# State-space layer: the inputs' products ahead of the output scalings; layer norms that subtract the mean first

## What is computed

```python
def _layer_norm(x, g, b):
    mu = jnp.mean(xf, -1, keepdims=True)
    var = jnp.mean(jnp.square(xf - mu), -1, keepdims=True)
    return ((xf - mu) * lax.rsqrt(var + LN_EPS)) * g + b

def _ssd_mixer(h, ...):
    z, xBC, dt = jnp.split(h @ in_w, ...)
    xBC = jax.nn.silu(_causal_depthwise_conv(xBC, conv_w, conv_b))
    xs, Bm, Cm = jnp.split(xBC, ...)
    y = _ssd_chunked(xs * dt[..., None], dt * A, Bm, Cm)
    y = y + xs * D_skip[:, None]
    y = y * jax.nn.silu(z)
    yg = yg * lax.rsqrt(jnp.mean(jnp.square(yg), -1) + RMS_EPS)     # 8 groups of 512 channels
    return (yg * norm_g) @ out_w
```

## Time and profile before

| | |
|---|---|
| three runs | 3546.73, 3548.98, 3554.34 us; median 3548.98 |
| the profiled execution | 3549.42 us, its span 3547.6 us, granted TensorE clock 0.995 |
| TensorE matmul / weight load busy | 97% / 95% |
| VectorE, ScalarE, GpSimd busy | 78%, 56%, 17% |
| DMA | 197 GB/s mean |

### The profile page before, as it was taken

How to read it: one execution, slowest core, us unless ns; L and a number is a source line. 1 busy time by engine, 2 the same in 40 slices (tenths; PEclk the granted TensorE clock), 3 DMA queues, 4 the chain that set the end, 5 groups by cost and what they waited for, 6 DMA issues and landing times.

```text
span 3547.6 us, 68240 instructions
## 1 busy us (share of the span) xinstructions
PE 3447.0 (97%) x27858; PEld 3381.8 (95%) x27858; DVE 2783.1 (78%) x4529; ACT 1987.5 (56%) x3204; POOL 587.2 (17%) x546
## 2 busy tenths in 40 slices
PE   7999999999999999999999999999999998999997
PEld 7999999999999998999999999999999998999997
DVE  7788888577797887877888887898989867666665
ACT  6555546566547676565555546665656746434344
POOL 2111112111113011131111112231313300000000
PEclk9999999999999999999999999999999999999999
DMA  6555556444465444655555565556464543555552
GB/s 239 217 197 219 217 227 231 176 155 179 165 251 203 172 169 173 267 185 218 201 221 202 208 262 180 178 175 230 171 233 169 186 169 146 210 189 199 204 190 107
DMA packets 113688, 699.61 MB, mean 197 GB/s; under 512 B 13216, under 2 KB 29792, under 8 KB 31456
## 3 DMA queue, kind: packets, MB, share of 16 engines
q1 hardware_dynamic: 104128, 685.14, 52.2%
q10 hardware_dynamic: 8784, 8.46, 1.0%
q0 software_dynamic: 464, 1.64, 0.1%
HBM read 684.64 MB, written 2.16 MB: 194 GB/s over the span
## 4 chain that ended last, share of the span: by engine, by line
PE 49%; DVE 13%; ACT 6%; issue 2%; DMA 1%; POOL 1%; DVEq 0%; SPq 0%; POOLq 0%; ACTq 0%
PE g L446 15%; PE g L448 15%; PE g L447 15%; DVE w_lo L1594 4%; ACT w_hi L1026 2%; DMA w_raw<-in_slots 1%; POOL scratch L2409 1%; DVE vec L2095 1%; DVE rstd L2095 1%; PE turn_bank L485 1%; DVE scratch L1659 1%; DVE scratch L2121 0%; DVE scratch L2129 0%; PE norm_bank L459 0%; DVE h L2225 0%
## 5 line engine op out<-in xcount | busy, mean ns | idle before, releaser
L1594 DVE TENSOR_TENSOR w_lo<-w_raw,w_hi 128x1024 fp32r<-128x1024 f32 x1088 | 1337.0, 1232 | 433.9 <-ACT w_hi L1026 423.1
L1026 ACT ACTIVATE w_hi<-w_raw 128x1024 fp32r<-128x1024 f32 x1088 | 1129.6, 1053 | 873.2 <-PE g L448 761.7
L446 PE MATMUL g<-p_hi,w_hi 128*128 128x256 f32 x4576 | 1318.0, 288 | 36.4 <-DVE w_lo L1594 23.2
L448 PE MATMUL g<-p_hi,w_lo 128*128 128x256 f32 x4576 | 1296.2, 283 | 0.0
L447 PE MATMUL g<-p_lo,w_hi 128*128 128x256 f32 x4576 | 1296.2, 283 | 0.0
L446 PE MATMUL g<-q_hi,w_hi 128*128 128x256 f32 x3408 | 980.0, 288 | 5.7 <-DVE w_lo L1594 2.2
L448 PE MATMUL g<-q_hi,w_lo 128*128 128x256 f32 x3408 | 964.0, 283 | 0.0
L447 PE MATMUL g<-q_lo,w_hi 128*128 128x256 f32 x3408 | 963.8, 283 | 0.0
L446 PEld LDWEIGHTS g<-p_hi,w_hi 128*128 128x128 f32 x4576 | 879.1, 192 | 46.1 <-DVE w_lo L1594 32.7
L447 PEld LDWEIGHTS g<-p_lo,w_hi 128*128 128x128 f32 x4576 | 879.3, 192 | 1.4
L448 PEld LDWEIGHTS g<-p_hi,w_lo 128*128 128x128 f32 x4576 | 879.0, 192 | 0.0
(11 more groups left out here) (445 smaller groups left out, 3929.2 us busy)
## 6 DMA issues: line engine op xcount, KB each, us to landing
w_raw<-in_slots SPq DMA_DIRECT2D x640, 1024.0 KB, 4.9
scratch<-scratch SPq DMA_DIRECT2D x128, 64.0 KB, 4.9
scratch<-s_rows ACTq DMA_DIRECT2D x16, 256.0 KB, 3.4
con<-s_rows ACTq DMA_DIRECT2D x16, 256.0 KB, 5.1
h<-in_x SPq DMA_DIRECT2D x4, 512.0 KB, 6.2
out_h<-h SPq DMA_DIRECT2D x4, 512.0 KB, 2.6
sq<-in_p POOLq DMA_DIRECT2D x4, 256.0 KB, 3.0
con<-in_consts SPq DMA_DIRECT2D x1, 832.0 KB, 10.7
```

Of the source, the lines that this page charges most:

```text
L446: pe.matmul(g, wh, hi[:, k], start=n == 0, stop=False)
L448: last = pe.matmul(g, wl, hi[:, k], start=False, stop=n == len(ks) - 1)
L1026: act.activation(w_hi[k % SPLIT][:, cols], raw[MAIN_AT[k] % RAW][:, cols], ACT.Copy).then_inc(hi_ready, 1)
L1594: dve.tensor_tensor(w_lo[k % SPLIT][:, cols], raw[MAIN_AT[k] % RAW][:, cols], w_hi[k % SPLIT][:, cols], SUB).then_inc(lo_ready, 1)
```

## The change

It has two parts.

1. In `s_group` on VectorE, step 6 now runs `s_inputs` and the clamp first and `s_scale_y` behind them, and step 7 runs `s_y_lo` behind its own `s_inputs` and clamp, no longer at its head. This holds for groups 1 to 7.
2. In `layer_norm`, the subtraction comes first and takes the mean straight from `rope_bank`. Five tiles are subtracted between the variance and the wait for `rstd`. Then each tile is multiplied by `rstd`; tiles 5 to 15 are subtracted (with a wait for its end) right before. The one product of mean and `rstd` is gone, and `low` runs one tile behind where it ran two behind.

```diff
+LN_AHEAD = 5
...
         def s_group(g):
             for n in range(10):
-                if g and n == 7:
-                    s_y_lo(g - 1)
                 begin()
...
                 lo_half(1)
-                if g:
+                if g and n < 6:
                     s_previous(g - 1, n)
                 if 4 <= n <= 7:
                     s_inputs(g, n - 4)
...
                     s_clamp(n, s_z[:, n - 6])
+                if g and n > 5:
+                    s_previous(g - 1, n)
+                if g and n == 7:
+                    s_y_lo(g - 1)
...
             dve.tensor_tensor(rsn[:, 1], bN[:, 0:SEQ], rsn[:, 0], SUB).then_inc(ln_var, 1)
+            for n in range(LN_AHEAD):
+                link(dve.tensor_tensor(h[:, n], h[:, n], bR[:, 0:SEQ], SUB))
             factor()
-            link(dve.tensor_tensor(rsn[:, 2], bR[:, 0:SEQ], rstd[:], MUL))
...
             for n in range(DT):
-                link(dve.tensor_tensor(h[:, n], h[:, n], rstd[:], MUL))
-                dve.tensor_tensor(h[:, n], h[:, n], rsn[:, 2], SUB).then_inc(ln_z, 1)
-                if w == 0 and n > 1:
-                    low(n - 2)
+                if n >= LN_AHEAD:
+                    link(dve.tensor_tensor(h[:, n], h[:, n], bR[:, 0:SEQ], SUB))
+                dve.tensor_tensor(h[:, n], h[:, n], rstd[:], MUL).then_inc(ln_z, 1)
+                if w == 0 and n:
+                    low(n - 1)
             if w == 0:
-                low(DT - 2)
                 low(DT - 1)
```

## The result

The changed kernel takes **3556.3 us** (median of 11 runs, 3552.4 to 3560.7); the kernel before takes 3549.0 in the same session (11 runs, 3546.7 to 3554.3). The ratio is **1.0021, 95% interval 1.0014 to 1.0029**, that is 5 to 10 us slower. The forecast was 3555.7 us, between 3551.0 and 3559.5, and +6.7 us. The profiled execution has a span of 3552.1 us, where that of before has 3547.6: 4.5 us more.

The account below looks back on a forecast made before the run. TensorE, 97% busy, was taken as the bound, with ScalarE's chain from the scalings pacing the state-space layer. Part 1 +7.0, first norm +1.2, last norm -1.6: +6.6, rounded up to +6.7, so 3555.7 us, range 3551.0 to 3559.5.

Parts of the forecast that it names:

- The stall and what replaces it: State-space layer: TensorE's seven 1.52 us stalls at `turn_bank` go; about 2.9 us at step 3 without projection instead of 0.5.
- The scalings' customer: Step 6: ScalarE waits for the scaled tiles, so it and the decay-row loads behind it start 1.36 us later.
- The collision moves along: Step 6, VectorE against GpSimd: the input product loses the 0.49 us and the scalings get it back.
- The four boundaries without projection: Between groups: the chain arrives 0.96, 1.18, 1.01 and 1.36 us later, together 4.5 us.
- less the idle time at step 1: Boundaries without projection: VectorE's idle 0.40, 0.18, 0.35 and 0 us at step 1 is taken off the 1.36 us delay.
- The two with a projection: After groups 2 and 4: TensorE waits for VectorE's copies, so each boundary adds 1.36 us, together 2.7.
- After group 7: Boundary behind the last group: TensorE starts 0.15 us behind the copy, 0.2 us earlier than before.
- The low part at nothing: Step 7: moving `s_y_lo` costs nothing, hidden by VectorE's wait at step 8; otherwise 1.14 us at each group.
- The first norm: Part 2, first layer norm: last `q_hi` about 20.8 us after the variance starts, two late tiles in 2.39; +1.2 us.
- The last norm: Part 2, last layer norm: 11.70 us from `rstd` on instead of 13.26, all on the path to the end; -1.6 us.
- The first: Rival: ScalarE's chain has at least 2.9 us of slack between scalings and step 3, giving 3538 us; chance 0.10.
- The third: Rival: chain closed on VectorE and ScalarE through `w_hi` at step 1, nothing absorbed; +9.1 us, 3558.1 us; chance 0.20.

Follow-up runs that it names:

- e4: Kernel before with VectorE's step 6 running scalings, then input products, ahead of the second half of `w_lo`: +3.0 us, ratio 1.0007.
- e7: Kernel before with the scalings ahead of both halves of `w_lo` at step 6 and the products ahead of the second: -2.0 us, ratio 0.9993.
- e3: Kernel before with VectorE's step 6 running input products, then scalings, ahead of the second half of `w_lo`: -2.1 us, ratio 0.9992.
- e5: e1 with the low part back at the head of step 7; against the kernel before: 3555.1 us, ratio 1.0015.
- e2: The change without its `s_group` part, only the layer norms changed; against the kernel before: 3547.3 us, ratio 0.9997.
- e1: The change without its `layer_norm` part, only the state-space layer changed; against the kernel before: 3556.7 us, ratio 1.0026.
- e10: e4 with the 1 MB weight load held until the decay rows have landed; against the kernel before: 3540.8 us, ratio 0.9979.
- e6: Kernel before with a layer norm that subtracts two tiles ahead of `rstd` and runs `low` two behind: 3546.4 us, ratio 0.9992.
- e8: e7 with the layer norm of e6; against the kernel before: 3544.3 us, ratio 0.9985.
- e11: e8 with e10's hold on the weight load; against the kernel before: 3537.1 us, ratio 0.9967.
- e9: Kernel before with the 1 MB weight load of step 6 delayed to just ahead of the decay-row fetch: 3567.8 us, ratio 1.005.
- e12: The changed kernel with the weight load of step 7 held until the decay rows have landed; against the kernel before: 3554.3 us, ratio 1.0017.

## Why the prediction was right

- **The stall and what replaces it.** Right. The stall's rows are gone and the output product waits 2.24, 2.24, 2.23 and 1.30 us at the four boundaries without projection; the last is the one ahead of which the clock had fallen. I had put it at about 2.9 with the restart; from start to start it is 2.5 at the first three.
- **The scalings' customer.** Right to 0.01: the fetch is issued 31.28 us after the output product for 29.93, +1.35 where the text had 1.36. e4 and e7, where the scalings come sooner, are the other side of it (28.79 and 28.51).
- **The collision moves along.** Right for this order: 0.83 for the product and 1.67 for the scalings. The product ends at 2325.78, just behind GpSimd's (2323.86 and 1.77 us, to 2325.63), so the trace agrees with the rule of the Trainium skill ("SBUF — State Buffer", "Who interferes with whom"). But the place behind a half of `w_lo`, to which the prediction tied it, is not the condition. In e3 and e4 the copy stands directly ahead; e3's product starts just ahead of GpSimd's and is not hit, nor are its scalings behind it, while e4's scalings, which run beside GpSimd's product, are (step 6, first e3, then e4):

```profile
2323.25 0.34 DVE L2116 TENSOR_SCALAR scratch<-rstd,vec 128x256 f32<-128x256 f32 x1
2323.30 0.90 POOL L2508 TENSOR_TENSOR vec<-vec,sin_b 128x256 f32<-128x256 f32 x1 [4.70 <-ACT sin_b L1072]
2324.41 1.66 DVE L2129 SCALAR_TENSOR_TENSOR scratch<-scratch,vec,rsn 128x256 f32<-128x256 f32 x4
...
2322.89 2.15 DVE L2129 SCALAR_TENSOR_TENSOR scratch<-scratch,vec,rsn 128x256 f32<-128x256 f32 x4
2322.93 1.03 POOL L2508 TENSOR_TENSOR vec<-vec,sin_b 128x256 f32<-128x256 f32 x1 [4.69 <-ACT sin_b L1072]
```

- **The four boundaries without projection.** Sum 3.8 for 4.5. The step that is off is "less the idle time at step 1". The true slack is the landing-to-product time less 31.5: 0.88, 0.64, 0.82 and 0.46, not 0.40, 0.18, 0.35 and 0; some of it lies behind step 1. The slack is 2.8 in sum where 0.93 was taken, an error of 1.9 us. Of this, 1.2 were given back by things that the sum didn't have: the fetch, taken as it was (3.13 us), changed by +0.36, +0.84, +0.06 and -0.31, and the fallen clock put the last issue 0.3 later. At boundary 3: 1.35 + 0.84 - 0.64 = 1.55, as measured. That the two errors cancel is luck.
- **The two with a projection.** +1.19 and +1.11 for 1.36 each: the 1.35 of the later issue, less 0.12 and 0.22 by which the fetch happened to be shorter. The first wait is now at the projection's first tile, not at the fifth that I had read.
- **After group 7.** -0.34 for -0.2, but not where it was forecast. The tile of the earlier trace rows starts 42.81 us behind the output product, for 42.80 before: nothing is gained there, because the fetch of this group took 3.57 us for 3.23. In e5, where it took 3.29, the tile starts at 42.56, which is the -0.2 of the text. The -0.34 arises behind it, mostly at the norm's last mean product, ahead of which TensorE waited 0.17 us before and doesn't now, and 0.1 of it belongs to part 2, in e2 as well. So the agreement of this number is luck too.
- **The low part at nothing.** Right (e5: same issue of the fetch).
- **The first norm.** Right: from the variance (2946.42) to the last `q_hi` (2967.22) it is 20.80 us, the 20.8 of the text, and two late tiles take 2.38 for 2.39.

```profile
2946.42 0.42 DVE L2220 TENSOR_TENSOR rsn<-norm_bank,rsn 128x256 f32<-128x256 f32 x1 [0.78 <-ACT rsn L1443]
...
2967.22 0.59 ACT L1449 ACTIVATE q_hi<-h,vec 128x256 fp32r<-128x256 f32 x1
...
2971.61 0.36 PE L448 MATMUL g<-q_hi,w_hi 128*128 128x256 f32 x1 [2.32 <-DVE scratch L2309]
```

- **The last norm.** -1.7 for -1.6.
- **The rivals.** The first (slack that I don't see) fell: there were 0.5 to 0.9 us a boundary where 2.9 were needed. The third comes nearest in part: its closed chain is there, but it runs through the fetch and the output product, not through `w_hi` at step 1, and the slack did absorb a part.

The sum of the terms as measured in the trace is +5.4 us, the forecast +6.7, and the medians say +7.4. The profiled execution is one of several, and two things differ from one to the next: the fetches, between 3.2 and 5.9 us, and the granted clock. In groups 1 to 7 it falls once in the trace of the change, three times in that of e1 and never in that of before; over the 11 runs of the change the three slowest (3558.7 to 3560.7) have a mean clock of 0.992 to 0.993, the three fastest (3552.4 to 3553.9) 0.994 to 0.995.

The prediction was right in its mechanism and somewhat lucky in its number, and the same picture failed on e4 and e7, where it expected 8 us: it took the fetch for a constant, and the change of order moved the fetch into the load's way.

## What to carry to other kernels

Before an operation is moved ahead of another to end a stall, ask who else waits for the one that is pushed back, and follow that chain around to the engine that bounds: here 1.36 us on ScalarE's side were worth more than 1.52 us of TensorE's stall. A small DMA whose landing is on the chain is to be looked at with the bulk transfers beside it: list for every variant the time from the bulk load's issue to its issue and from its issue to its use, and hold the bulk load back if it has buffers to spare. It was this one line on SyncE that turned +3.0 into -8.2 us. And a wait of TensorE that grows past what stood there before can cost more than its length: look at the granted clock behind it.

## What was not expected of the hardware

- A fetch of 256 KB takes 3.3 us when the 1 MB load was issued 5.8 us ahead of it or held behind it, and 5.1 to 5.9 in the mean of a kernel when it was issued 0.7 to 1.3 us ahead (single ones 4.5 to 6.6). It doesn't get a share of the bandwidth while the load moves: its first bytes come when those of the load have ended or nearly so. With the load 2.5 us ahead they come 1.5 to 1.7 us after the issue for 1.0, and the fetch takes 3.2 to 4.9. A load issued 1.1 to 1.5 us behind it costs little or nothing in most groups (3.34 in the mean with it in the kernel before, 3.30 without it in e10).
- After waits of TensorE of 1.8 to 2.3 us at the output product the granted clock fell from 2.4 to 1.2 GHz in some groups and not in others of the same trace (behind one of three such waits in the change, three of three in e1). It never fell there in before, e2, e3, e6, e8, e10 and e11, whose longest wait in these groups is below 1.5 us.
- The chain from landing to output product, over ScalarE, VectorE and GpSimd, repeats to within 0.04 us (31.50 to 31.54) in the nine kernels in which it is the bound (e8, e9 and e12 beside those of the table).
